# Feature rows and gated rows at another byte distance from the weights in each phase of a three-layer forward pass

## What is computed

```
for each layer:
    h = modulate(rmsnorm(x), shift, scale)
    x = x + g_a * (mixer(h @ w_in) @ w_out)
    h = modulate(rmsnorm(x), shift2, scale2)
    x = x + g_f * ((act(h @ w_up_a) * (h @ w_up_b)) @ w_down)
out = rmsnorm(x)
```

## Time and profile before

| | us |
|---|---|
| median of three runs | 1454.56 |
| span of the profiled execution | 1454.6 |
| TensorE matmul busy | 1403.6 (96%) |
| TensorE weight loads busy | 1172.3 (81%) |
| VectorE busy | 848.5 (58%) |
| GpSimd busy | 840.2 (58%) |
| ScalarE busy | 659.0 (45%) |

### The profile page before, as it was taken

The page is one execution under the profiler, slowest core; times in us unless marked ns, Lnnn a source line. Parts: engine busy times, 40 slices in busy tenths (PEclk is TensorE's granted clock), DMA queues, the critical chain, the costliest instruction groups (busy, mean ns, idle before and its releaser), DMA issues.

```text
span 1454.6 us, 21621 instructions
## 1 busy us (share of the span) xinstructions
PE 1403.6 (96%) x8272; PEld 1172.3 (81%) x8272; DVE 848.5 (58%) x1638; ACT 659.0 (45%) x1070; POOL 840.2 (58%) x672
## 2 busy tenths in 40 slices
PE   5999999999999999999999999999999999999998
PEld 2978789999988888546878888888888866888887
DVE  3798667776676689688675333321126768554522
ACT  3555665455453133684342232232226386544442
POOL 1533427998864444675444554544446530699997
PEclk9999999999999999999999999999999999999999
DMA  9748516777775652010445555533333320365664
GB/s 365 288 164 309 195 50 212 248 258 241 243 259 194 202 192 80 31 44 15 174 174 182 195 202 185 193 122 96 102 107 102 110 94 16 118 200 188 187 187 135
DMA packets 71207, 242.01 MB, mean 166 GB/s; under 512 B 7488, under 2 KB 12992, under 8 KB 70720
## 3 DMA queue, kind: packets, MB, share of 16 engines
q1 hardware_dynamic: 68688, 236.63, 48.1%
q10 hardware_dynamic: 2416, 4.00, 0.9%
HBM read 238.50 MB, written 1.05 MB: 165 GB/s over the span
## 4 chain that ended last, share of the span: by engine, by line
PE 52%; DVE 4%; ACT 1%; issue 0%; POOL 0%; DVEq 0%; ACTq 0%
PE bank L731 9%; PE bank L737 9%; PE bank L732 9%; PE bank L593 8%; PE bank L594 4%; PE bank L584 2%; PE bank L586 1%; PE bank L585 1%; PE bank L592 1%; PE cond_a L1124 1%; PE bank L1124 1%; DVE h_both L2239 1%; PE bank L1132 1%; PE cond_a L1185 1%; PE bank L1144 1%; PE cond_b L1144 1%
## 5 line engine op out<-in xcount | busy, mean ns | idle before, releaser
L2010 POOL TENSOR_TENSOR w_lo<-raw,w_hi 128x512 fp32r<-128x512 f32 (+2 forms) x610 | 776.8, 1302 | 581.1 <-ACT w_hi L1466 572.9
L1466 ACT ACTIVATE w_hi<-raw 128x1024 fp32r<-128x1024 f32 (+3 forms) x300 | 307.9, 1029 | 582.7 <-PE bank L737 375.2
L731 PE MATMUL bank<-h_both,w_hi 128*128 128x512 f32 (+1 forms) x1000 | 323.1, 340 | 1.2 <-ACT w_hi L1466 1.2
L732 PE MATMUL bank<-h_both,w_hi 128*128 128x512 f32 (+1 forms) x1000 | 322.5, 340 | 0.0
L731 PEld LDWEIGHTS bank<-h_both,w_hi 128*128 128x128 f32 x1000 | 188.3, 188 | 22.9 <-ACT w_hi L1466 1.4
L732 PEld LDWEIGHTS bank<-h_both,w_hi 128*128 128x128 f32 x1000 | 188.3, 188 | 21.3
L737 PE MATMUL bank<-h_both,w_lo 128*128 128x512 f32 (+1 forms) x1000 | 198.1, 340 | 0.0
L737 PEld LDWEIGHTS bank<-h_both,w_lo 128*128 128x128 f32 x1000 | 160.4, 188 | 21.4 <-POOL w_lo L2010 0.2
L2124 DVE CUSTOM_DVE_ANT_0 ada_junk<-ada_w,cond_a 128x1024 bf16<-128x1024 f32 x128 | 153.5, 1215 | 15.1 <-DVE work L2687 8.1
L2106 DVE TENSOR_TENSOR hidden_both<-work,hidden_both 128x256 fp32r<-128x256 f32 (+1 forms) x66 | 58.5, 886 | 135.0 <-ACT hidden_both L1547 135.0
L593 PE MATMUL bank<-h_both,w_hi 128*128 128x512 f32 x345 | 122.8, 394 | 0.0
(11 more groups left out here) (487 smaller groups left out, 2544.1 us busy)
## 6 DMA issues: line engine op xcount, KB each, us to landing
raw<-in_up SPq DMA_DIRECT2D x132, 512.0 KB, 3.6
ada_w<-in_ada SPq DMA_DIRECT2D x128, 512.0 KB, 4.5
raw<-in_down SPq DMA_DIRECT2D x48, 448.0 KB, 3.5
raw<-in_out SPq DMA_DIRECT2D x24, 512.0 KB, 3.5
raw<-in_down SPq DMA_DIRECT2D x24, 512.0 KB, 3.6
raw<-in_in SPq DMA_DIRECT2D x24, 512.0 KB, 3.5
arena<-in_ada SPq DMA_DIRECT2D x16, 512.0 KB, 11.8
raw<-in_uq SPq DMA_DIRECT2D x12, 384.0 KB, 3.1
```

The lines of the kernel that those rows point to most:

```text
L731: pe.matmul(out, w_h[:, k - k0], hi[:, k, cols], start=(k == 0), stop=False)
L732: pe.matmul(out, w_h[:, k - k0], lo[:, k, cols], start=False, stop=False)
L1466: act.activation(part_slot(w_hi, f, u), raw_slot(f, u), ACT.Copy).then_inc(s["rounded"], 1)
L2010: pool.tensor_tensor(part_slot(w_lo, f, u)[:, a:b], raw_slot(f, u)[:, a:b], part_slot(w_hi, f, u)[:, a:b].bitcast(F32), ALU.subtract).then ...
```

## The change

Both tensors get room to the right, `h_both` 128 elements and `hidden_both` 64, and every phase takes its rows from an offset of its own in it. `scratch`, which shares the room of `h_both`, starts 16 elements into it. Producers and consumers of a phase use the same offset. The scratch for descriptors shrinks from 2048 to 1024 bytes; it lies at address 0, so everything behind it moves down by 1024 bytes. `h_both` then begins 128 bytes past a multiple of 512, `hidden_both` stays at 384. No instruction is added or removed.

```
+H_ROOM = 128
+HIDDEN_ROOM = 64
+MIXING = (80, 0, 32)
+UP_AT = (176, 96, 208)
+DOWN_AT = (200, 48, 192)
+OUT_AT = (224, 16, 240)
...
-        with nc.sbuf_tensor("hidden_both", [P, 2, KF, TOK], F32R) as hidden_both:
-            hidden_hi, hidden_lo = hidden_both[:, 0], hidden_both[:, 1]
-        stack.enter_context(nc.sbuf_tensor("arena_end", [P, ARENA], F32))
-        with nc.sbuf_tensor("scratch", [P, 2 * KD * TOK], F32) as scratch:
-        h_both = sbr("h_both", [P, 2, KD, TOK])
+        with nc.sbuf_tensor("hidden_both", [P, HIDDEN_ROOM + 2 * KF * TOK], F32R) as hidden_room:
+        def hidden(n):
+            a = DOWN_AT[1] if n == 1 else 0
+            both = hidden_room[:, a:a + 2 * KF * TOK].rearrange("p (a k t) -> p a k t", a=2, k=KF)
+            return both, both[:, 0], both[:, 1]
+        stack.enter_context(nc.sbuf_tensor("arena_end", [P, HIDDEN_ROOM + ARENA], F32))
+        with nc.sbuf_tensor("scratch", [P, H_ROOM + 2 * KD * TOK], F32) as scratch_room:
+            scratch = scratch_room[:, OUT_AT[1]:OUT_AT[1] + 2 * KD * TOK]
+        h_room = sbr("h_both", [P, H_ROOM + 2 * KD * TOK])
+        def rows_from(a):
+            both = h_room[:, a:a + 2 * KD * TOK].rearrange("p (a k t) -> p a k t", a=2, k=KD)
+            return both, both[:, 0], both[:, 1]
+        def features(name):
+            if name[:-1] in ("up", "out"):
+                at = (UP_AT if name[:-1] == "up" else OUT_AT)[int(name[-1])]
+                return rows_from(at if name in ("up1", "out1") else 0)
+            return rows_from(MIXING[1 if name in ("in1", "vra", "vrb") else 2 if name in ("ckv", "cq") else 0])
...
-        def columns(t0, t1):
-            return slice(t0 - 24, t1 - 24) if t0 == L0 else slice(t0, t1)
+        def columns(name, t0, t1):
+            at = {"u": UP_AT, "d": DOWN_AT, "o": OUT_AT}[name[0]][int(name[-1])]
+            return slice(at, at + LAT) if t0 == L0 else slice(t0, t1)
...
-    nc = bacc.Bacc("TRN2", target_bir_lowering=False, num_devices=1, dynamic_dma_scratch_size=2048)
+    nc = bacc.Bacc("TRN2", target_bir_lowering=False, num_devices=1, dynamic_dma_scratch_size=1024)
```

More of the change, by code:

```diff
@@ L675, in first_linear @@
             def first_linear(gate):
+                _, h_hi, h_lo = features("va_gates")
                 f = ph["va_gates"]
@@ L719, in linear @@
                 f = ph[name]
-                both = h_both if both is None else both
+                both = features(name)[0] if both is None else both
                 hi, lo = (both[:, 0], both[:, 1]) if hi is None else (hi, lo)
                 n, parts = t1 - t0, f.parts
-                cols = columns(t0, t1) if name[:-1] in ("up", "down", "out") else slice(t0, t1)
+                cols = columns(name, t0, t1) if name[:-1] in ("up", "down", "out") else slice(t0, t1)
                 def high_then_low(u, k0, k1):
@@ L809, in token_linear @@
                 f = ph[name]
-                hi, lo = (h_hi, h_lo) if hi is None else (hi, lo)
+                hi, lo = features(name)[1:] if hi is None else (hi, lo)
                 pair = 2 if f.steps == 2 else 1
@@ L839, in values_and_steps @@
                 f = ph["vra"]
+                _, h_hi, h_lo = features("vra")
                 for u, (k0, k1) in enumerate(f.ranges):
@@ L1056, in out_first @@
                 order = (4, 5, 6, 7, 0, 1, 2, 3)
+                h_both, h_hi, h_lo = features("out0")
+                late = columns("out0", L0, L1)
                 def one(u, k):
@@ L1088, in out_ahead @@
                 f = ph["out2"]
+                h_both, late = features("out2")[0], columns("out2", L0, L1)
                 def some(u, k0, k1):
@@ L1367, in ffn @@
                 linear(f"up{n}", t0, t1, gate=next_h(), early=True)
-                linear(f"down{n}", t0, t1, K=KF, both=hidden_both,
+                linear(f"down{n}", t0, t1, K=KF, both=hidden(n)[0],
                        gate=lambda k: pe.wait_ge(s["hid_done"], KF * n + k + 1))
@@ L1527, in round_h @@
             def round_h(src, t0, t1):
+                h_hi = features("va_gates")[1]
                 for k in range(KD):
@@ L1534, in shift_h @@
             def shift_h(n, which, both):
+                name = (("va_gates", "in1", "ckv")[n], f"up{n}")[which]
+                h_hi = features(name)[1]
+                late = None if both else columns(name, L0, L1)
                 for k in range(KD):
@@ L1546, in round_hidden @@
                 act.wait_ge(s["hid_in"], KF * n + i + 1)
-                act.activation(hidden_hi[:, i, columns(t0, t1)], work[:, i % 3, t0:t1], ACT.Copy).then_inc(s["hid_round"], 1)
+                act.activation(hidden(n)[1][:, i, columns(f"down{n}", t0, t1)], work[:, i % 3, t0:t1], ACT.Copy).then_inc(s["hid_round"], 1)
             def softplus_part(ready, x):
@@ L1772, in _ @@
                     act.wait_ge(s["taken"], shared.stop)
-                    act.activation(h_hi[:, 4:8, late], y_att, ACT.Copy).then_inc(s["ya_round"], 1)
+                    act.activation(features("out0")[1][:, 4:8, columns("out0", L0, L1)], y_att, ACT.Copy).then_inc(s["ya_round"], 1)
                 if h == 2:
@@ L1785, in _ @@
                 act.wait_ge(s["ml_gate"], h + 1)
-                act.activation(h_hi[:, h, late], gated_m[:, h, :], ACT.Copy).then_inc(s["ml_round"], 1)
+                act.activation(features("out0")[1][:, h, columns("out0", L0, L1)], gated_m[:, h, :], ACT.Copy).then_inc(s["ml_round"], 1)
             act.wait_ge(s["ml_y"], MH)
@@ L1903, in round_y @@
                 act.wait_ge(s["h_work"], h_count[0] + k + 1)
-                act.activation(h_hi[:, k, :], y1[:, k, :], ACT.Copy).then_inc(s["h_round"], 1)
+                act.activation(features("out1")[1][:, k, :], y1[:, k, :], ACT.Copy).then_inc(s["h_round"], 1)
             for q in range(3, 2 * RH):
@@ L2038, in round_group @@
                 pool.wait_ge(s["h_work"], 3 * KD + p + 1)
[L2039 removed]
+                pool.tensor_scalar(features("out1")[1][:, p, :], y1[:, p, :], 1.0, None, ALU.mult).then_inc(s["h_round"], 1)
             def gate_product(i):
@@ L2224, in norm @@
                 sides = ([(0, L0, 1)] if both else []) + [(L0, L1, 0)]
+                name = (("va_gates", "in1", "ckv")[n], f"up{n}")[which]
+                _, h_hi, h_lo = features(name)
+                late = None if both else columns(name, L0, L1)
                 def scaled(k):
@@ L2527, in mlstm @@
                 dve.wait_ge(s["ya_round"], 1)
+                _, h_hi, h_lo = features("out0")
+                late = columns("out0", L0, L1)
                 low(h_lo[:, 4:8, late], y_att, h_hi[:, 4:8, late]).then_inc(s["ya_low"], 1)
@@ L2558, in attention @@
             def attention(m, a0, heads, scale, sinks, tile0):
+                _, h_hi, h_lo = features("out0" if sinks else "out2")
+                late = columns("out0" if sinks else "out2", L0, L1)
                 if sinks:
@@ L2694, in hidden_low @@
                 dve.wait_ge(s["hid_round"], KF * n + i + 1)
-                low(hidden_lo[:, i, columns(t0, t1)], work[:, i % 3, t0:t1], hidden_hi[:, i, columns(t0, t1)]).then_inc(s["hid_done"], 1)
+                own = columns(f"down{n}", t0, t1)
+                low(hidden(n)[2][:, i, own], work[:, i % 3, t0:t1], hidden(n)[1][:, i, own]).then_inc(s["hid_done"], 1)
             def ffn0():
@@ L2903, in lower @@
                     dve.wait_ge(s["h_round"], h_count[0] + k + 1)
+                    _, h_hi, h_lo = features("out1")
                     low(h_lo[:, k, :], y1[:, k, :], h_hi[:, k, :]).then_inc(s["h_split"], 1)
```

3 lines of the change are left out of this document (1 added, 2 removed).

## The result

The changed kernel is slower: 1463.48 us (median of four runs, 1461.98 to 1468.45) against 1453.85 for the kernel before in the same comparison, ratio 1.0056 (95% interval 1.0038 to 1.0074; the bare medians would give 1.0066). Forecast were 1442.2 us and a range up to 1462. A run's time is 1.8 us above the span of its profile (1462.3 and 1460.5 us in the profiled run), so the profiled run of before, with its span of 1454.6, lay some 2 us above its median; between the two profiles lie 5.9 us.

What follows compares the result with a forecast made beforehand. TensorE was taken as the bound, its time the number of matmuls times their spacing, which depends on row-to-weight distance. The terms summed to -12.4 us: 1454.6 to 1442.2 us (chance 0.50), 8-in-10 range 1420 to 1462.

Steps and rivals of the forecast that it cites:

- first rival: All phases: the reads do not disturb each other, stationary-tile swap makes the surcharge, no distance matters; 1454.6 us, chance 0.17.
- the row at 448 fell to a surcharge of 6.7 and stayed: down1, 256 to 448: time beyond one column per cycle falls from 13.3 to 6.7 ns a matmul; -3.5 us.
- up1's term: up1, 256 to 384: surcharge of 10 ns, the middle between 13.3 and 6.7; -3.5 us (-7.0 to +7.0).
- the upper bound: Phases sent to distances no long stream showed: surcharge at most 20 ns a matmul, from uk and uv.
- up0: up0, 160 to 192: surcharge of 10 ns, spacing 118.6 to 116.7 ns; -2.0 us (-5.6 to +8.5).
- up2 and out2: Pairs of 2 x 256 and 256 columns from 346.0 to 340.0 ns in up2 (-2.0 us), 333.3 in out2 (-0.7).
- down2 was put at 0: down2, 160 to 0: a pair at 226.7 and 120.0 would be 346.7 ns, so no change (-2.0 to +2.2 us).
- The zeros for in1, out1, ckv and cq: Phases sent to distances 0, 64 and 128, with no row near: spacing kept, 0 us (-6.6 to +6.6).
- the sign that the prediction had named: VectorE's or ScalarE's instructions on the rows changing their means: distance acts beyond TensorE and the sum missed a part.
- second rival: in1, out1, down1, down2, ckv: near distance 0 both reads fall to the higher level; 1464.8 us, chance 0.21.
- third rival: All streams settle on the lowest level, a surcharge of 6.7 ns; 34.2 us gained, 1420.4 us, chance 0.12.
- the cover in up2: up2: GpSimd's weight splitting, 2.69 us a unit, stays below TensorE's 2.72 at 340.0 ns pairs; costs nothing.

Runs made afterwards that it cites:

- map_alone: A kernel of matmuls only, 88 groups of 48 at many distances and four column counts, no other engine working; gave spacings per distance, no ratio to the kernel before.
- two_alone: Changed kernel with offsets giving every phase the distances of the kernel before, except up1 at 384 and down1 at 448; ratio 1.0062 to the kernel before.
- undo_two: Changed kernel with up1's and down1's rows put back at distance 256; ratio 1.001 to the kernel before.
- scratch_alone: Kernel before with the descriptor scratch cut from 2048 to 1024 bytes as the only edit; ratio 0.9999.
- changed_again: The changed kernel run once more, unaltered, beside later versions; ratio 1.0061 to the kernel before.
- up0_112: Changed kernel with 512-column phases at 0 or 256, pairs at 160, up0 and down0 at 112; median 1452.56 against 1456.40 us, ratio 0.9977.

## Why the prediction was wrong

**What held.** TensorE's spacing was what the change acted on, the counts stayed, the descriptor scratch was worth nothing (0.9999), and the spacing does depend on the distance. The first rival, no influence of the distance, is refuted most plainly by map_alone, 226.7 to 240.0 ns for 512 columns with TensorE by itself. The Trainium skill ("TensorE: Matmul & The Clock Gate", "Step-by-step: what each phase is for") has loading weights take no read bandwidth from the running matmul, so that no distance would matter; here it does, by up to 13.3 ns a matmul in map_alone, and the measurements decide. The levels as multiples of 6.67 ns came again: 113.3, 120.0, 226.7, 233.3, 240.0; though steady spacings between them exist (117.8, 228.9, 234.3).

**The step that failed** is the one of down1 and up1: "the row at 448 fell to a surcharge of 6.7 and stayed" was a row of 256 columns, and I carried its surcharge over to 512 columns. At 448 256 columns have a surcharge of 6.7 and 512 columns one of 20. up1's term, a surcharge of 10 at 384, leaned on the same rows of 256 columns; it measured 19.1. The prediction had one row with both shapes at a distance, 256, where they happen to agree at 13.3, and took from it that the surcharge belongs to the distance alone. The only other rows of 512 columns, uk's and uv's at 224 and 288, stood at 20; they were in the prediction as the upper bound, and should have been the value taken. All seven phases with 512 columns that the change moves leave 256, where they sat lower than the only other rows of that shape. The two terms came out at +9.3 us instead of -7.0, and that is the miss: two_alone reproduces the loss with them alone, undo_two takes it away.

**Other terms.** up0 was near in size (-2.4 for -2.0) by luck: not one level between, but two levels, one after the other, and against two_alone's 124.3 us at the old distance the changed kernel's 124.1 gains next to nothing. up2 and out2 (-2.7 forecast, +1.0 measured) fell with the same step, as the part of 2 x 256 columns behaves as 512 do. down2 was put at 0, from two levels of the single shapes; the order of the shapes has a level of its own (353.3 instead of 346.7). The zeros for in1, out1, ckv and cq were right to 0.3 us, which is luck as well: the change happened to send the two long ones to 0 and 64, the lowest levels of the map for 512 columns beside 240, and ckv, which rose by 5 ns, has 72 matmuls. VectorE showed the sign that the prediction had named: its low gated rows of 256 tokens took 884 ns in the mean before (867 in scratch_alone, 889 in two_alone) and 970 after (954 in undo_two, 917 in changed_again). No wait of TensorE names these rows, so it cost nothing that the profiles show; whether the rows' new place or the work beside them does it was not tried.

**The second rival** had the sign and the size (1464.8 us) with the wrong place. Its mechanism, a higher level near distance 0, is refuted for 512 columns: in1 at 0 stayed at 226.8, and 0 is their best distance. The higher level lies nearly everywhere else. The third rival's lowest level of 220.0 for 512 columns was found at no distance.

**What is late next.** I looked for the cover in up2 and found GpSimd; there no gain came, so it was not put to the test. Where TensorE did get faster, in up0 and down0, the loop of load, round and split became the limit in stretches, and by the two profiles new waits took back about two thirds of the gain in up0_112. The prediction had not costed that for the first layer. The same may explain why undo_two came out at 1.001 and not 0.997: the first layer's gain in spacing is cut by waits and by up0's second level, and the kernel before may itself run at the lower level of 160; how much each took in the timed runs was not separated.

**Open.** Why 256 bytes, why 16-column levels, and what in the start of a stream picks one, the runs don't tell; that two reads fall into step is still an argument and not shown. How often a kernel takes which level in its timed runs is unknown, as a kernel has one profile, the changed one two. Whether the level can be forced in a full kernel wasn't tried.

## What to carry to other kernels

A stream of matmuls in which each brings a new stationary tile has a cost that depends on the byte distance between the rows and the weights, modulo 256, and on the number of columns: measure it for each shape, and never carry it from one shape to another. For float32r here, 512 columns want distance 0 or 256 and 256 columns want 112, or 192 with the risk of its second level (117.8). Before spending on a faster engine, look at what waits for it and how close its supply follows: here, by the profiles, a third of the gain in up0 and down0 arrived and new waits took the rest.

## What the runs showed of the hardware that was not expected

- With TensorE alone, 512 float32r columns take from 226.7 to 234.7 ns at distances that are multiples of 16 bytes (236.7 at 240 behind some streams), and up to 240.0 at others; 256 columns from 113.3 to 120.1, and up to 126.7. The map repeats after 256 bytes at the distances tried.
- It is the distance that counts and not the rows' own place: with the stream's place held and the stationary tile moved, 256 columns go from 120.0 to 113.5 or 118.0 ns.
- The order of distances differs by shape: 192 is best for 256 columns (113.3) and poor for 512 (233.3).
- A distance can have several steady spacings (256 columns at 192: 113.3 and 117.8, at 160: 117.3 and 118.7; 512 at 240: 226.7, 233.3 and 236.7), kept for up to a thousand matmuls; some short waits changed them, others did not.
- Two shapes in alternation have a spacing that is not the sum of their own (353.2 against 346.7 ns at distance 0).
